# Retention beside the first product's columns, two-column products in token halves, and a rotation on GpSimd

## The reference, cut to what matters

```
proj = h @ ret_w_in                       # 1024 x 6144: q, k (4 heads x 256), v, g (4 heads x 512)
q, k = rope(q), rope(k) * dk ** -0.5
o = ((q @ k.T) * decay) @ v               # per head, causal; the chunked form of the source, unrolled
o = (o - mean(o)) * rsqrt(var(o) + eps)   # per head
mix = (silu(g) * o) @ ret_w_out           # 2048 x 1024
h = layer_norm(ALPHA * h + mix)
h = layer_norm(ALPHA * h + moe(h))        # router logits h @ router_w first, then the experts
... the same with sparse attention in place of the retention (its w_out is 1024 x 1024)
... block 2: rms_norm; product A (3 columns of 512), product B (9: q, k, v of 3 groups, q and k rotated),
    gates (4 columns); attentions; y = gates * (oa @ w_a_out) + gates * (ob @ w_b_out)
    x = x + rms_norm(y @ w_mix_out); x = x + rms_norm(conv_gelu_gate(rms_norm(x) @ w_up) @ w_down)
```

## Time and profile before

| | |
|---|---|
| runs | 1596.59, 1602.97, 1605.67 us (median 1602.97) |
| profiled execution | 1598.54 us, its span 1596.5 us |
| busy | TensorE 1426 us (89%), VectorE 1166 (73%), ScalarE 928 (58%), GpSimd 12 (1%) |
| mean granted TensorE clock | 0.943 |
| weights and inputs read | 340.8 MB |

### The profile page before, as it was taken

The page is one execution under the profiler, slowest core; times in us unless marked ns, Lnnn a source line. Parts: engine busy times, 40 slices in busy tenths (PEclk is TensorE's granted clock), DMA queues, the critical chain, the costliest instruction groups (busy, mean ns, idle before and its releaser), DMA issues.

```text
span 1596.5 us, 18892 instructions
## 1 busy us (share of the span) xinstructions
PE 1426.2 (89%) x7388; PEld 1191.5 (75%) x7388; DVE 1166.4 (73%) x1443; ACT 928.1 (58%) x1091; POOL 11.6 (1%) x8
## 2 busy tenths in 40 slices
PE   6999695999999697599779999996989998799997
PEld 5887485788887576377668888875767887599976
DVE  4753656899999865366589999987678556567862
ACT  3435332989888543156268989873535564455651
POOL 0000001000000000000100000000000000000000
PEclk9999895999999898799789999998999999799999
DMA  9555051899999736200359999993544434455541
GB/s 327 188 185 200 12 181 56 309 383 389 384 398 397 272 94 216 94 3 10 117 197 386 384 378 397 399 390 120 163 133 150 156 135 131 137 165 190 185 146 39
DMA packets 127278, 343.17 MB, mean 215 GB/s; under 512 B 8956, under 2 KB 15692, under 8 KB 110668
## 3 DMA queue, kind: packets, MB, share of 16 engines
q1 hardware_dynamic: 117472, 327.37, 56.5%
q10 hardware_dynamic: 9708, 14.47, 2.8%
HBM read 340.77 MB, written 1.05 MB: 214 GB/s over the span
## 4 chain that ended last, share of the span: by engine, by line
PE 67%; DVE 15%; ACT 6%; issue 4%; DMA 3%; PEld 2%; PEldq 1%; ACTq 0%; DVEq 0%
PE PS L1064 16%; PE PS L567 14%; PE PS L506 13%; PE PS L496 7%; DVE wlo L463 4%; PE PS L548 3%; ACT whi L457 3%; PE PS L1103 2%; PE PS L1053 2%; DMA raw<-in_moe_w_down 2%; PE PS L1138 2%; DVE rope_t L757 1%; DMA raw<-in_moe_w_gate 1%; PE PS L1134 1%; PE PS L1832 1%
## 5 line engine op out<-in xcount | busy, mean ns | idle before, releaser
L463 DVE TENSOR_TENSOR wlo<-raw,whi 128x2048 fp32r<-128x2048 f32 x314 | 704.1, 2268 | 157.6 <-ACT whi L457 153.1
L457 ACT ACTIVATE whi<-raw 128x2048 fp32r<-128x2048 f32 x314 | 589.0, 1896 | 42.2 <-PE PS L548 14.9
L1064 PE MATMUL PS<-whi,xg 128*128 128x512 f32 x512 | 205.5, 401 | 0.0
L1064 PE MATMUL PS<-wlo,xg 128*128 128x512 f32 x512 | 200.4, 391 | 0.0
L567 PE MATMUL PS<-whi,th 128*128 128x512 f32 (+1 forms) x384 | 154.7, 403 | 4.2 <-DVE tl L665 4.2
L567 PE MATMUL PS<-wlo,th 128*128 128x512 f32 (+1 forms) x384 | 151.3, 394 | 0.0
L567 PE MATMUL PS<-whi,tl 128*128 128x512 f32 (+1 forms) x384 | 151.3, 394 | 0.0
L1064 PEld LDWEIGHTS PS<-whi,xg 128*128 128x128 f32 x512 | 96.4, 188 | 18.5
L1064 PEld LDWEIGHTS PS<-wlo,xg 128*128 128x128 f32 x512 | 96.3, 188 | 18.5
L1064 PE MATMUL PS<-whi,hT 128*128 128x512 f32 x256 | 100.5, 392 | 2.8 <-DVE hT L1283 2.8
L496 PE MATMUL PS<-th,whi 128*128 128x256 f32 x352 | 99.6, 283 | 1.4 <-DVE tl L665 1.4
(11 more groups left out here) (387 smaller groups left out, 2433.8 us busy)
## 6 DMA issues: line engine op xcount, KB each, us to landing
raw<-in_moe_w_gate SPq DMA_DIRECT2D x64, 1024.0 KB, 7.6
raw<-in_moe_w_up SPq DMA_DIRECT2D x64, 1024.0 KB, 8.4
raw<-in_moe_w_down SPq DMA_DIRECT2D x64, 1024.0 KB, 7.8
raw<-in_w_in SPq DMA_DIRECT2D x32, 1024.0 KB, 5.2
raw<-in_ret_w_in SPq DMA_DIRECT2D x24, 1024.0 KB, 5.2
raw<-in_w_up SPq DMA_DIRECT2D x20, 1024.0 KB, 5.1
raw<-in_w_down SPq DMA_DIRECT2D x10, 1024.0 KB, 5.0
raw<-in_ret_w_out SPq DMA_DIRECT2D x8, 1024.0 KB, 5.0
```

Source lines behind the costliest of these rows:

```text
L457: nc.scalar.activation(s.whi[:, high, 0:kc, 0:wide], s.raw[:, slot, 0:kc, 0:wide], ACT.Copy).then_inc(s.hi_done, 1)
L463: nc.vector.tensor_tensor(s.wlo[:, slot, 0:kc, 0:wide], s.raw[:, slot, 0:kc, 0:wide], s.whi[:, high, 0:kc, 0:wide], ALU.subtract).then_inc ...
L1064: last = nc.tensor.matmul(PS[:, bank, :], stationary(c), w[:, q, c, :], start=(start and c == 0 and k == 0), stop=(stop and c == KC - 1 an ...
```

## The change

1. **Retention.** `l_ret_in` becomes a steady product with `ret_beside_tensor`, `_scalar` and `_vector` after its blocks: q and k are turned after blocks 5, 7, 9, 11; the scores of head 0 after 12, values of head h and scores of h + 1 after 13, 15, 17, 19; roots and norms at 14 to 20; gates at 18, 20, 22; heads 0 to 2 are turned after 19, 21, 23, head 3 beside the first block of the output product. Each gate column is evacuated with Silu. The three barriers and the two at the turns go. Angles move from column 7 to 5. `ret_sd` lies at `gb_at`.
2. **Token halves.** `l_ret_out` is cut into an opening part (`open_tensor`: heads 0 and 1, both columns, blocks walked as before) and a last part of four blocks; `l_down` into eight and four. `halves_tensor` walks the last part's blocks (also all of `l_nsa_out`, `l_b_out`, `l_mix`) first for token half 0, then for half 1, and the half's residual, norm, transposes (`out_and_norm_*`, `joined_half`, `mixed_half`, `gain_of_half`) stand beside the other half. Blocks count as used in the second pass alone. The logits of half 0 come before the transposes of half 1.
3. **GpSimd** rotates B's columns 0 to 5 (`rope_pool`), in place of `rotate_b` on VectorE; the transposes wait on `b_rotated`.
4. One more down block is split before the last gate (`ff_side`).

```diff
-        ret_sd = A("ret_sd", [P, 2, 3, P], at=th_at)
+        ret_sd = A("ret_sd", [P, 2, 3, P], at=gb_at)
-        l_ret_out = linear(2, [4, 4, 4, 4], plain(a["ret_w_out"][0]))
+        l_ret_open = linear(2, [4, 4], plain(a["ret_w_out"][0][0:D, :]), opens=True)
+        l_ret_out = linear(2, [4, 4], plain(a["ret_w_out"][0][D:2 * D, :]))
+        def halves_tensor(pe, l, xh, xl, bank, c0=0, opened=False, free=None, between=None, low=same):
+            nk = len(l.groups)
+            for tt in range(TT):
+                for n in range(nk * l.n):
+                    j, kb = n // nk, n % nk
+                    b = l.b0 + n
+                    if tt == 0:
...
+                        pe.wait_ge(lo_done, b + 1)
+                    for c in range(l.groups[kb]):
...
+                    if tt == 1:
+                        last.then_inc(block_used, 1)
+                    elif kb == nk - 1:
+                        last.then_inc(half_product, 1)
+                    if between is not None:
+                        between(tt, n)
+        def rope_pool(o, x, cos, sin, heads, half):
...
+            o.wait()
+            for i, (u, v) in enumerate(((x1, c), (x2, s), (x2, c), (x1, s))):
+                o(nc.gpsimd.tensor_tensor(t[i], u, v, ALU.mult))
+            o.wait()
+            o(nc.gpsimd.tensor_tensor(x1, t[0], t[1], ALU.subtract))
+            o(nc.gpsimd.tensor_tensor(x2, t[2], t[3], ALU.add))
+        def ret_values_tensor(pe, h):
+            pe.wait_ge(ret_decayed, h + 1)
+            pe.wait_ge(acc_free, 2 * (4 + h + 1))
+            if h == 0:
+                pe.wait_ge(ret_copied, 4)
+            else:
+                pe.wait_ge(ret_out, 2 * h)
...
+        def ret_beside_tensor(pe, n):
+            if n in (5, 7, 9, 11):
+                ret_turn_tensor(pe, (n - 5) // 2)
+            if n in (13, 15, 17, 19):
+                ret_values_tensor(pe, (n - 13) // 2)
+            if n == 12:
+                ret_scores_tensor(pe, 0)
+            if n in (13, 15, 17):
+                ret_scores_tensor(pe, (n - 11) // 2)
+            if n in (19, 21, 23):
+                ret_out_turn_tensor(pe, (n - 19) // 2)
+        def out_and_norm_vector(dve, st, o, l, layer):
+            for i in (2, 3):
+                split_lo(dve, sweep_first, l.b0 + i, 0)
+            residual_half(dve, o, l, 0, 0)
+            split_lo(dve, sweep_first, l.b0 + 4, 0)
+            residual_half(dve, o, l, 0, 1)
+            dve.wait_ge(params_in, 16 * st.params)
+            norm_half(dve, o, 4 * layer, 0)
+            residual_half(dve, o, l, 1, 0)
+            split_lo(dve, sweep_first, l.b0 + 5, 0)
+            half_turn_vector(dve, 1 + 2 * layer, 0)
+            residual_half(dve, o, l, 1, 1)
+            norm_half(dve, o, 4 * layer, 1)
     (ff_side)
+            split(eng, sweep_first, l_down_open.b0 + 2, 0)
             gate(5)
     (tensor)
-            product(l_ret_in, th, tl)
-            turn(by_column(ret_proj), 16)
-            retention_tensor(pe, st)
-            end()
-            turn(lambda tt, c: ret_o[:, tt, c // 4, (c % 4) * P:(c % 4 + 1) * P], 16)
-            linear_tensor(pe, l_ret_out, ret_oTh, ret_oTl)
+            steady_tensor(pe, l_ret_in, th, tl, lambda n: ret_beside_tensor(pe, n))
...
+            open_tensor(pe, l_ret_open, ret_oTh, ret_oTl, in_order, heads_turned, ret_low,
+                        lambda j: 2 * (l_ret_out.n0 + j - 1), beside_open)
+            pe.wait_ge(ret_o_lo, RET_H)
+            out_and_norm_tensor(pe, l_ret_out, ret_oTh, ret_oTl, 0, DC, True, ret_low)
     (scalar, around l_mix)
+            for i in range(2):
+                split_hi(act, sweep_first, l_mix.b0 + i, 0)
+            half_turn_scalar(act, 5, 0)
+            split_hi(act, sweep_first, l_mix.b0 + 2, 0)
+            half_turn_scalar(act, 5, 1)
             params(act, st, norm_params(a["post_mix_g_2"][0], a["pre_ffn_g_2"][0]))
             early_table(ACT.Sqrt)
+            split_hi(act, sweep_first, l_mix.b0 + 3, 0)
             for tt in range(TT):
+                square_of_half(act, l_mix, tt, 0, in_turn(l_mix), mix)
+                split_hi(act, sweep_first, l_up.b0 + tt, 0)
+                square_of_half(act, l_mix, tt, 1, in_turn(l_mix), mix)
+                root_half(act, 10 + tt, tt)
+                square_half(act, 10 + tt, tt, mix)
+                root_half(act, 11 + tt, tt)
                 half_turn_scalar(act, 6, tt)
     (vector, after l_b_out)
+            gain_of_half(dve, o, l_mix, 0, 0, in_turn(l_mix), mix_t)
+            split_lo(dve, sweep_first, l_up.b0, 0)
+            mixed_half(0)
+            gain_of_half(dve, o, l_mix, 1, 0, in_turn(l_mix), mix_t)
+            split_lo(dve, sweep_first, l_up.b0 + 1, 0)
+            half_turn_vector(dve, 6, 0)
+            mixed_half(1)
     (gpsimd)
+            pool.wait_ge(rotated, RET_H + 2)
+            o = Order(pool, pool_order)
+            for j in range(6):
+                pool.wait_ge(acc_free, 2 * (l_b_in.n0 + j + 1))
+                for tt in range(TT):
+                    rope_pool(o, b_proj[:, j, tt, :].rearrange("p (h b d) -> p h b d", h=4, b=2),
+                              trig[:, 0, tt, 32:96], trig[:, 1, tt, 32:96], 4, 64)
+                o.wait()
+                pool.drain().then_inc(b_rotated, 1)
```

More of the change, by code:

```diff
@@ L532, in linear_side, with same, open_tensor @@
             take(l.n - 1, 0)
-        def down_tensor(pe):
-            nk = len(l_down.groups)
-            pe.wait_ge(acc_free, 2 * (l_up.n0 + 9))
-            for n in range(nk * l_down.n):
-                j, kb = n // nk, n % nk
-                b = l_down.b0 + n
-                if j == 0:
-                    pe.wait_ge(ff_lo, kb + 1)
+        def same(c):
+            return c
+        def open_tensor(pe, l, xh, xl, bank, ready=None, low=same, free=None, beside=None):
+            nk = len(l.groups)
+            for n in range(nk * l.n):
+                j, kb = n // nk, n % nk
+                b = l.b0 + n
+                if kb == 0 and free is not None:
+                    pe.wait_ge(acc_free, free(j))
+                if j == 0 and ready is not None:
+                    ready(kb)
@@ L552, in down_tensor @@
-                last.then_inc(block_used, 1)
+                    for c in range(KC):
+                        for i, (x, w, k) in enumerate(((xh, whi, b % HIGHS), (xh, wlo, b % RAWS), (xl, whi, b % HIGHS))):
+                            at = low(KC * kb + c) if i == 2 else KC * kb + c
+                            last = nc.tensor.matmul(PS[:, bank(j, tt), :], x[:, at, tt * P:(tt + 1) * P],
+                                                    w[:, k, c, :], start=(kb == 0 and c == 0 and i == 0), stop=False)
@@ L642, in root_vector, with half_turn_tensor @@
             o.then(nc.vector.reciprocal(small[:, cols], small[:, cols]))
-        def half_turn_tensor(pe, k, source, ready):
-            for tt in range(TT):
+        def half_turn_tensor(pe, k, source, ready, halves=range(TT)):
+            for tt in halves:
                 ready(tt)
@@ new lines, in ret_scores_tensor @@
+        def ret_scores_tensor(pe, h):
+            pe.wait_ge(ret_copied, 3 if h < 2 else 4)
+            if h:
+                pe.wait_ge(ret_decayed, h)
+            for i, (kt, qt) in enumerate(ret_pairs()):
+                for c in range(2):
+                    last = nc.tensor.matmul(PS[:, 4, i * P:(i + 1) * P], ret_qkT[:, 8 + 2 * h + c, kt * P:(kt + 1) * P],
+                                            ret_qkT[:, 2 * h + c, qt * P:(qt + 1) * P], start=(c == 0), stop=(c == 1))
+            last.then_inc(ret_scores, 1)
@@ new lines, in ret_normed_vector, with ret_gate_vector @@
+        def ret_normed_vector(dve, o, h):
+            dve.wait_ge(norm_root, h + 1)
+            o.then(nc.vector.reciprocal(small[:, 8:10], small[:, 8:10]))
+            for qt in range(TT):
+                nc.vector.tensor_scalar(ret_o[:, qt, h, :], PS[:, 6 + qt, :], small[:, 2 * qt:2 * qt + 1],
+                                        small[:, 8 + qt:9 + qt], ALU.subtract, ALU.mult).then_inc(ret_out, 1)
+        def ret_gate_vector(dve, h):
+            dve.wait_ge(acc_free, 2 * (8 + h + 1))
+            dve.wait_ge(ret_out, 2 * (h + 1))
+            for qt in range(TT):
+                last = nc.vector.tensor_tensor(ret_o[:, qt, h, :], ret_o[:, qt, h, :], ret_proj[:, 8 + h, qt, :],
+                                               ALU.mult)
+            last.then_inc(ret_gated, 1)
@@ L2352, in beside_b_in @@
                 for j in turns.get(n, ()):
[L2353 removed]
+                    pe.wait_ge(b_rotated, j + 1)
                     pe.wait_ge(att_out, 2 * A_H)
@@ L2524, in _ @@
             early_table(ACT.Sqrt)
-            squares = squares_by_column(lambda j: PS[:, 4 + 2 * j:6 + 2 * j, :], ff_sq, down_squared)
-            linear_side(act, l_down, split_hi, lambda j, turn: squares(j), ahead=False)
+            for n in range(3, 12):
```

(3 more changed lines are left out.)

480 lines of the change are left out of this document (274 added, 206 removed).

## The result

The changed kernel takes 1546.08 us as the median of four executions (1544.84 to 1550.85), the kernel before 1602.53 (four, 1596.59 to 1605.67): a ratio of 0.9657, 95% interval 0.9623 to 0.9692. The profiled execution took 1545.94 us, its span 1544.1 us, so its span is 52.4 us shorter; the forecast sum was 53.1. The forecast of the median was 1550 us, in a range of 1537 to 1565. One execution of the kernel before, among the eleven taken beside experiments 7 and 9, took 3646.62 us where the others took 1597 to 1606, and is left out of their ratios.

A forecast was written before the change was run, and what follows sets the result against it. Gains lie between products, where TensorE has work but waits; expert layers stay untouched. Terms 20.0 + 16.4 + 7.5 + 4.0 + 3.2 + 2.0 = 53.1 take 1598.54 to 1545.4; 4.4 for the median gives 1550 us, range 1537 to 1565.

The forecast's parts named there:

- Retention: Between the first two products: moving the steps beside product blocks saves 20.0 us, after 0.4 us taken for stalls.
- only the two long barrier waits go: Retention's lower bound: only TensorE's two longest barrier waits, 6.7 and 2.2 us, are saved, 8.9 us.
- Rival 1: Retention steps stall the product through a late root or rotation; only 8.9 us comes out, 1561 us; chance 0.13.
- no stretch of over 2 us without product matmuls: Sign for the retention, between the first block and the last block of the output product.
- Warm transposes and cold logits, 12.0: Each norm-and-router stretch: second half's norm, transposes and logits take 12.0 us behind the product; saving 8.2 us each.
- Rival 3: Clock: logits stay warm throughout and the mix tail is at its other bound; 1540 us; chance 0.08.
- the four waits of the earlier trace: B input product: TensorE's waits for VectorE's rotation go once GpSimd rotates; 7.5 us saved.
- the collision: B input product: VectorE operations reading two SBUF tensors wait up to 0.7 us for GpSimd, 1.4 us per step pair.
- The order of the queues: Behind the mix product: queued work delays the second half's gain some 4 us, tail 13.7 us; joins still save 4.0.
- The 5.6 us per block: Mix product: each of its six blocks takes 5.6 us, 33.6 us together.
- The -2.0 behind the product: Behind the down product: only one half's work remains, saving a gain (0.7) and a pass (1.3), 2 us.
- The -3.2: Down product: TensorE's 3.2 us wait for the third block's low split goes, as it is made before the last gate.

The follow-up runs named there:

- experiment 7: Changed kernel with only the 14 unread matmuls around the second half's transposes in the router stretches, none behind the logits: 1546.26 us, ratio 0.9647.
- experiment 9: Changed kernel with the reordered queues behind the mix product and the fourth mix block split before parameters and table load, no extra matmuls: 1542.37 us, ratio 0.9632.
- experiment 2: Changed kernel with the retention's steps behind the first product's last block, same order, no barriers, no product beside them: 1582.42 us, ratio 0.9883.
- experiment 3: Changed kernel with the products ahead of the routers walked block by block for both token halves, first half's transposes behind the last block: 1560.46 us, ratio 0.9731.
- experiment 6: Changed kernel with unread matmuls in TensorE's gaps of both router stretches (8, 6, 44 and 8): 1545.74 us, ratio 0.9636.
- experiment 8: Changed kernel with the edits of experiment 4 and experiment 6, and the fourth mix block split before parameters and table load: 1542.76 us, ratio 0.9621.
- experiment 4: Changed kernel with ScalarE's and VectorE's queues behind the mix product reordered, second half's squares first, second up block's low split later: 1544.00 us, ratio 0.9639.
- experiment 5: Changed kernel with each of the rotation's four GpSimd multiplies made three times, 168 operations instead of 72: 1600.54 us, ratio 0.9975.
- experiment 1: Changed kernel with the rotation of B's six columns back on VectorE: 1555.69 us, ratio 0.9712.

## Why the prediction was right

**Retention.** The step was right, and its term was 1.7 us low. It took off 0.4 us for stalls of which there were none; the moved steps take 22.7 us and not 23.3, as the scores were priced at 2.94 us for two heads and take 2.68; and the first product's own matmuls take 136.8 us instead of 137.5, since the slow matmuls at its start, 0.43 us apart instead of 0.23, end 1.6 us earlier in this profile (at 20.5 instead of 22.2). The last 0.6 is therefore luck. The prediction's lower bound, "only the two long barrier waits go" (8.9 us), assumed that the rest of the stage would cost what it did. Experiment 2 shows that for this order of steps it does not: without the product beside it, it takes 12 us more than the old stage. Rival 1 (a late root or rotation) did not come: TensorE waits on neither. One of the prediction's signs, no stretch of over 2 us without product matmuls, did not fit its own sum: a head's values and the next one's scores stand between two blocks for 3.9 us.

**Norm and router.** "Warm transposes and cold logits, 12.0" gave 12.7 and 13.3. The norm's chain was right to 0.1 us. The part that failed is "warm transposes": they took 1.40 us in the first layer and 1.98 in the second where warm ones take 0.87. "Cold logits" was right, in 5.33 us instead of 5.1, for the second 24, which are on the path; the first 24 run warm behind the product, in time that TensorE would have idled. By the norm's own stretches (experiment 3) the halves are worth somewhat less than the 7.5 and 6.9 of the table. Rival 3 had the clock's 5 us as its price; experiments 6 to 8 made the logits warm, and by the medians nothing came of it.

**GpSimd.** The term was right by its mechanism (the four waits of the earlier trace rows) and 0.8 us low. The forecast of the steps came true: two of them in 14.6 us. The prediction bounded the collision by one GpSimd operation, 0.7 us, twice in a pair of steps. VectorE's eight small operations lose 0.5 us each, one after the other, so here the wait is paid once per operation and not twice per pair, and in that one place it costs about 5 us where 1.4 were allowed. That the collision costs TensorE nothing was right, but only just: VectorE is busy 11.1 of the 12 us from 1178 on, and TensorE waits 0.3 us for it right behind. The Trainium skill ("SBUF — State Buffer", section "SBUF: two separate sides") says that the pair goes for the whole instruction to whichever starts first; these rows agree (0.35 us becomes 0.84 on average, within one 0.7 us GpSimd operation). Of VectorE's operations it names those with two SBUF inputs or in a two-port mode; the reduction of one SBUF tensor, not slowed (1.22 us in both kernels), agrees, and under which of the two the small tensor_scalar falls (0.65 instead of 0.17) these rows do not tell. The price of the GpSimd operation, forecast 0.71 to 0.8, is 0.93 (66.6 us for 72) with the collisions in it. The prediction called the 2.85 us row in line with the 4497 ns for 2048 elements of the Trainium skill ("GPSIMD Engine Reference", "Performance versus the Vector engine"); the row is 2.8 ns per element and that figure 2.2, and the measured row decides.

**Mix.** The order of the queues was read right and confirmed by experiment 4. The term was 0.7 us too large: the wait at the fourth block is 1.0 us and not 1.5, the tail 12.9 and not 13.7, and the six blocks took 35.5 us instead of 33.6. The 5.6 us per block was the weak step: the kernel before took 11.4 and 24.5 us for the same six, 35.9. Of these 1.9, 1.7 are the first 36 matmuls (10.1 us instead of 8.4), at a granted clock of 0.64 for their first 4.5 us; the prediction had taken 5.6 us for every block.

**Down product and end.** The -2.0 behind the product is right. The -3.2 is right by luck. The wait for the low split is gone, as forecast, but it had cost more than its 3.2 us: behind it the kernel before ran slow matmuls (columns as above, the granted clock is 0.58).

```profile
1537.10:1541.10 4.00, 3.96 (x11) 3.16 (x12) 4.00 (x2) 3.92 (x3) 0.00 (x0) 0.58 0.31 119
```

So the down product went from 65.2 us to 59.9, 5.3 less, of which the prediction had the wait alone. The up product ahead of it, the same 1056 matmuls, went from 125.9 to 128.1, which no edit explains, and the two cancel to -3.2.

**Sum.** The terms missed by +1.7, -0.7, -1.3, +0.8, -0.7, 0 and 0, and what the change does not touch became 0.2 longer: 52.7. The 0.3 to the 52.4 of the spans lie in short stretches that the table leaves out, 0.2 of it between the first layer's logits and its first expert matmul. The forecast of the median added the 4.4 us by which the shown median stood over the profiled execution; over four executions of the changed kernel that came to 0.1, so the 4.4 was scatter. That is why the median fell by 56.5 us, to 1546.08 and not to 1550.

## What to carry to other kernels

A stage between two products is worth what its engines idle there, and here it was hidden by a long product and a block of slack in each hand-over (less was not tried); the same steps without cover, barriers gone, lost time (experiment 2). A wait can cost more than its length: behind one of 3.2 and one of 2.0 us TensorE lost some 2 us more, at a granted clock of 0.58 and 0.57; behind the other three of experiment 1 the clock stayed at 1.00. A helper engine's price is a deadline: count its operations against the time until its result is asked for, and not against its speed (experiment 5). Behind a product read each in-order queue down to the instruction that the path needs: the splits ahead of it cost 3 us here, and moving them took a few lines.

## What the hardware showed that was not expected

**GpSimd slows VectorE's small operations the most.** 128x128 operations with two SBUF operands took 0.84 us instead of 0.35, eight in a row, while a 2.29 us split lost 0.4; in these rows each pays once, however small it is.

**The same product takes 2.5 us more or less from profile to profile.** The up product's first 8 us, behind the same idle time, ran at 0.50 and 0.79 in the changed kernel and at 0.62 and 1.00 with the rotation on VectorE. The second four us of each:

```profile
1353.70:1357.70 4.00, 4.00 (x29) 4.00 (x29) 1.49 (x1) 0.00 (x0) 0.00 (x0) 0.79 0.00 0
```

```profile
1362.70:1366.70 4.00, 4.00 (x37) 4.00 (x36) 1.43 (x1) 0.00 (x0) 0.00 (x0) 1.00 0.00 0
```

The up product takes 125.5 to 125.7 us in experiments 1, 8 and 9, 126.7 in 7, and 128.0 to 128.2 in the changed kernel and the five others. Between the two windows' profiles 1.2 us of the 2.5 arise in the first 66 matmuls; the rest is spread over the whole product (66 matmuls take 7.83 us against 7.74) at a granted clock of 1.00 in both, and its cause is open. That is 2.5 us of span for no edit of that part, as much as experiments 4, 7 and 9 were about; such edits can only be read by their own stretch and by several executions.

The B output product is another matter. Its first 4.5 us ran at 0.64 in the changed kernel and at 1.00 in the one before, behind the same wait of 2.5 us, but its first 36 matmuls take 10.0 to 10.2 us in the changed kernel and in all nine experiments. So it is not scatter among them, and what sets it apart from the kernel before is open.

**A warm clock can be bought and bring nothing that shows.** Experiment 6 raised the mean granted clock from 0.954 to 0.967 and left the time as it was, within what four executions can tell.
